# Two transformer blocks with a product-key expert layer: 32 instead of 16 of 128 first keys computed densely

## The reference, cut to what matters

```
q = (t @ wq).reshape(T, 8, 2, 128)          # 256 tokens, 8 heads, two halves
s1, s2 = q[:, :, 0] . k1, q[:, :, 1] . k2   # scores of 128 first and 128 second keys
v1, i1 = top_k(s1, 16); v2, i2 = top_k(s2, 16)
sc, pos = top_k(v1[..., :, None] + v2[..., None, :], 16)
idx = i1 * 128 + i2 at pos                  # expert number, of 16384
g = softmax(sc)
act = gelu(einsum('thkd,td->thk', u[idx], t))
out = einsum('thk,thkd->td', g * act, v[idx])
```

## Time and profile before

| | |
|---|---|
| three runs | 2838.87 us median (2834.85, 2838.87, 2839.47) |
| the profiled execution's own time | 2835.17 us |
| its span in the profile | 2833.4 us |
| busy share of the span | PE 85%, DVE 61%, ACT 50%, POOL 33% |
| granted TensorE clock, mean | 0.941 |
| HBM read | 809.09 MB |
| indirect gathers (queue q0) | 475.38 MB |

### The profile page before, as it was taken

One profiled execution on the slowest core, in us unless ns is written; L12 is line 12 of the kernel. 1 busy time (PEld: TensorE's weight loads), 2 busy tenths in 40 slices (PEclk: granted clock), 3 DMA queues, 4 the chain that ended last, 5 costly groups with the idle time before them and its releaser, 6 DMA issues.

```text
span 2833.4 us, 37176 instructions
## 1 busy us (share of the span) xinstructions
PE 2406.3 (85%) x14973; PEld 2079.6 (73%) x14973; DVE 1716.1 (61%) x2428; ACT 1421.4 (50%) x1692; POOL 926.2 (33%) x731
## 2 busy tenths in 40 slices
PE   8999999999999999999999677777766767777756
PEld 7887898888888788778888566666666666565654
DVE  4767564555456555577556877666647874444455
ACT  5567555544776444455554455444444444333443
POOL 6013150000000000432002646465446766344454
PEclk9999999999999999999999889898987778999977
DMA  7544404555445546334446999999999999999988
GB/s 229 190 142 153 137 16 146 165 195 193 150 133 185 183 129 223 119 119 161 156 162 227 380 374 403 410 400 413 406 409 381 402 385 413 415 398 412 416 347 337
DMA packets 209660, 751.84 MB, mean 265 GB/s; under 512 B 25133, under 2 KB 29449, under 8 KB 150857
## 3 DMA queue, kind: packets, MB, share of 16 engines
q0 software_dynamic: 74400, 475.38, 41.7%
q1 hardware_dynamic: 135088, 274.09, 28.2%
HBM read 809.09 MB, written 2.10 MB: 286 GB/s over the span
## 4 chain that ended last, share of the span: by engine, by line
DMA 28%; PE 21%; DVE 9%; issue 4%; POOL 4%; ACT 2%; POOLq 0%; DVEq 0%; ACTq 0%
DMA UROW<-in_peer_u_dram,WORK 20%; PE bank L2243 19%; DMA VROW<-in_peer_v_dram,WORK 7%; DVE BIG L2181 5%; POOL VROW L679 2%; POOL UROW L671 2%; PE bank L2898 1%; ACT VROW L1332 1%; DVE BIG L1741 0%; DVE WL L1441 0%; DMA UROW<-in_peer_v_dram,WORK 0%; DVE UROW L2181 0%; PE bank L2379 0%; ACT WH L799 0%; DVE WORK L1764 0%
## 5 line engine op out<-in xcount | busy, mean ns | idle before, releaser
L2898 PE MATMUL bank<-ID,VROW 128*128 128x128 f32 x3904 | 578.6, 312 | 373.6 <-ACT VROW L1332 373.4
L2181 DVE CUSTOM_DVE_ANT_0 BIG<-UROW,BIG 128x2048 f32<-128x2048 f32 x252 | 578.1, 2294 | 429.8 <-DMA UROW<-in_peer_u_dram,WORK 413.4
L2898 PEld LDWEIGHTS bank<-ID,VROW 128*128 128x128 f32 x3904 | 516.7, 161 | 429.1 <-ACT VROW L1332 421.9
L1332 ACT ACTIVATE VROW<-VROW,WORK 128x2048 f32<-128x2048 f32 x244 | 487.9, 2001 | 630.3 <-DMA VROW<-in_peer_v_dram,WORK 630.3
L2243 PE MATMUL bank<-HX,WH 128*128 128x512 f32 (+1 forms) x2784 | 759.5, 345 | 12.0 <-issue 4.8
L2243 PE MATMUL bank<-HX,WL 128*128 128x256 f32 x2128 | 595.5, 280 | 0.0
L671 POOL DMA_INDIRECT UROW<-in_peer_u_dram,WORK x256 | 340.2, 1329 | 631.3 <-DVE WORK L2181 408.3
L2243 PEld LDWEIGHTS bank<-HX,WH 128*128 128x128 f32 x2784 | 479.9, 189 | 84.1 <-issue 16.7
L1447 DVE TENSOR_TENSOR WL<-RAW,WH 128x1024 fp32r<-128x1024 f32 (+2 forms) x261 | 305.2, 1180 | 298.3 <-ACT WH L799 297.3
L2243 PE MATMUL bank<-WH,HX 128*128 128x512 f32 (+1 forms) x1472 | 453.1, 390 | 3.4 <-ACT BIG L742 2.5
L2243 PEld LDWEIGHTS bank<-HX,WL 128*128 128x128 f32 x2128 | 402.1, 189 | 0.1
(11 more groups left out here) (394 smaller groups left out, 2345.0 us busy)
## 6 DMA issues: line engine op xcount, KB each, us to landing
RAW<-in_w_in_odd_dram SPq DMA_DIRECT2D x64, 1024.0 KB, 5.3
RAW<-in_w_in_even_dram SPq DMA_DIRECT2D x48, 1024.0 KB, 5.3
RAW<-in_w_in_dram SPq DMA_DIRECT2D x44, 1024.0 KB, 5.0
RAW<-in_w_out_even_dram SPq DMA_DIRECT2D x16, 1024.0 KB, 5.1
RAW<-in_w_out_odd_dram SPq DMA_DIRECT2D x16, 1024.0 KB, 5.1
RAW<-in_w_out_dram SPq DMA_DIRECT2D x16, 1024.0 KB, 5.1
RAW<-in_peer_wq_dram SPq DMA_DIRECT2D x16, 1024.0 KB, 5.0
DROW<-in_peer_u_dram SPq DMA_DIRECT2D x32, 512.0 KB, 8.0
```

The lines of the kernel that those rows point to most:

```text
L1332: act.activation(v_buffer(n), v_buffer(n), ACT.Copy, scale=COEF[:, n:n + 1])\
L2181: dve.tensor_tensor_reduce(out=product, in0=UROW[:, b, :], in1=TT[m], op0=ALU.mult, op1=ALU.add, scale=1.0, scalar=0.0, accum_out=DOT[:, n ...
L2898: ins = pe.matmul(bank[c // 4][:, c % 4 * P:(c % 4 + 1) * P], v_buffer(n)[:, c * P:(c + 1) * P], ID[:, :], start=pick == 0 and c % 4 == 0, ...
```

## The change

`DENSE` becomes 32, so that experts with a first key of 96 or more (not 112) are computed densely and their rows aren't gathered. U_STEPS and V_STEPS become 128 each. The first dense steps lie on picks 2 to 115 (before: 2 to 108), the gate groups on 119 to 151 (112 to 155), the second dense steps on 155 to 233 (161 to 224). The search of block 1 takes 32 steps over picks 37 to 83, two in three picks, instead of one every second pick up to 99. ACTED has four parts instead of two, and takes BIG 4 to 12: the buffer JUNK is gone (the dot product now writes its product over the row), and the one-hots move from BIG into HT, whose first writing waits for the last dense dot. ACT waits for the searches ahead of the 17th and the 25th key, not the 9th. mix works in four parts instead of two. ADD_DENSE_AT, SUM_AT and SCALE_AT move from 108, 113 and 121 to 115, 119 and 124 picks into block 1 (236, 241, 249 to 243, 247, 252).

```diff
--- before.py
+++ after.py
@@ -44,7 +44,7 @@
 PICKS = PE_HEADS * PE_TOP
 ROWS_EACH, SECOND_ROWS = 4, 5
 V_LAG = 8
-DENSE = 16
+DENSE = 32
 KEPT = PE_KEYS - DENSE
 U_STEPS, V_STEPS = 4 * DENSE, 4 * DENSE
 GROUPS, IN_GROUP = 16, 16
@@ -52,7 +52,7 @@
 BATCH = 4
 N_PICKS = MT * PICKS
 ADD_AT = PICKS + 11
-ADD_DENSE_AT, SUM_AT, SCALE_AT = PICKS + 108, PICKS + 113, PICKS + 121
+ADD_DENSE_AT, SUM_AT, SCALE_AT = PICKS + 115, PICKS + 119, PICKS + 124
 ON_DVE = (N_PICKS - 7, N_PICKS - 5, N_PICKS - 4, N_PICKS - 2)
 TURNED = N_PICKS - 12
 BACK_AT = tuple(PICKS + 2 * g for g in range(4))
@@ -63,7 +63,6 @@
 TOP_STEPS = 8
 TOP_PLACES = (0, 1, 3, 4, 6, 8, 10, 12)
 TOP_LATER = (10, 20, 28)
-TOP_AT, TOP_EVERY = 37, 2
 TOP_INSIDE = TOP_STEPS
 GATES_AT = 116
 
@@ -73,10 +72,11 @@
     return {i: first + i * (last - first) // steps for i in range(steps)}
 
 
-U_AT = spread(U_STEPS + 1, 2, 109)
-G_TURN_AT = 110
-G_AT = spread(GROUPS, 112, 158)
-V_AT = spread(V_STEPS, 161, 226)
+TOP_BLOCK_1 = spread(4 * TOP_STEPS, 37, 85)
+U_AT = spread(U_STEPS + 1, 2, 116)
+G_TURN_AT = 117
+G_AT = spread(GROUPS, 119, 154)
+V_AT = spread(V_STEPS, 155, 234)
 G_PARTS_AT = G_TURN_AT + V_LAG + 1
 OH_AT = {g: v + V_LAG - 1 for g, v in G_AT.items()}
 MIX_AT = {g: v + V_LAG + 2 for g, v in G_AT.items()}
@@ -389,14 +389,14 @@
         GATE = WORK[:, 1024:1280]
 
         TT = [BIG[:, 2 * m:2 * m + 2, :].rearrange("p a b -> p (a b)") for m in range(MT)]
-        JUNK = BIG[:, 6:8, :].rearrange("p a b -> p (a b)")
         LNF = BIG[:, 0:2, :].rearrange("p a b -> p (a b)")
         UT = BIG[:, 15, :].rearrange("p (b n) -> p b n", b=2)
 
-        ACTED = [BIG[:, 4:6, :].rearrange("p a (j t) -> p (a j) t", t=T), BIG[:, 8:10, :].rearrange("p a (j t) -> p (a j) t", t=T)]
-        OH2 = BIG[:, 10:12, :].rearrange("p a b -> p (a b)").bitcast(BF16).rearrange("p (b t n) -> p b t n", b=2, n=P)
+        ACTED = [BIG[:, 4 + 2 * i:6 + 2 * i, :].rearrange("p a (j t) -> p (a j) t", t=T) for i in range((DENSE + 7) // 8)]
+        one_hot = HT[:, :, :].rearrange("p a b -> p (a b)").bitcast(BF16)
+        OH2 = one_hot[:, 0:4096].rearrange("p (b t n) -> p b t n", b=2, n=P)
         g_bf = BIG[:, 12:14, :].rearrange("p a b -> p (a b)").bitcast(BF16)
-        OH1 = g_bf[:, 0:2048].rearrange("p (b k t n) -> p b k t n", b=2, k=4, n=DENSE)
+        OH1 = one_hot[:, 4096:4096 + 8 * IN_GROUP * DENSE].rearrange("p (b k t n) -> p b k t n", b=2, k=4, n=DENSE)
         GATE_PARTS = g_bf[:, 2048:2816].rearrange("p (k t) -> p k t", k=3)
         I1T, I2T, IOTA_B = g_bf[:, 2816:3072], g_bf[:, 3072:3328], g_bf[:, 3328:3456]
         G_REST = BIG[:, 13, 768:1024]
@@ -1289,8 +1289,8 @@
             def dense_gelu(j):
 
                 act.wait_ge(s["d_m"], 4 * (j + 1))
-                if j == 8:
-                    act.wait_ge(s["tk_idx"], 4)
+                if j in (16, 24):
+                    act.wait_ge(s["tk_idx"], 4 if j == 16 else 8)
                 act.activation(ACTED[j // 8][:, j % 8, :], bank[6 + j % 2][:, 0:T], ACT.Gelu)\
                     .then_inc(s["d_act"], 1)
 
@@ -2124,6 +2124,9 @@
             def one_hots(g):
 
                 b, ts = g % 2, slice(IN_GROUP * g, IN_GROUP * (g + 1))
+                if g == 0:
+
+                    dve.wait_ge(s["d_m"], U_STEPS)
                 if g >= 2:
                     dve.wait_ge(s["g_g"], g)
 
@@ -2144,9 +2147,9 @@
                 dve.wait_ge(s["g_g"], g + 2)
                 dve.wait_ge(s["d_act"], DENSE)
                 gates_of = bank[6 + g % 2][:, 0:IN_GROUP * DENSE].rearrange("p (t a) -> p a t", a=DENSE)
-                for half in range(2):
-                    x = ACTED[half][:, :, IN_GROUP * g:IN_GROUP * (g + 1)]
-                    ins = dve.tensor_tensor(x, x, gates_of[:, 8 * half:8 * half + 8, :], ALU.mult)
+                for part in range(len(ACTED)):
+                    x = ACTED[part][:, :, IN_GROUP * g:IN_GROUP * (g + 1)]
+                    ins = dve.tensor_tensor(x, x, gates_of[:, 8 * part:8 * part + 8, :], ALU.mult)
                 ins.then_inc(s["g_mix"], 1)
 
             def root(m):
@@ -2177,8 +2180,7 @@
                 dve.wait_ge(s[f"u_row{b}"], 16 * (n // ROWS_EACH + 1))
                 if n >= 1:
                     dve.wait_ge(s["u_dot"], n)
-                product = UROW[:, b, :] if n < ROWS_EACH else JUNK
-                dve.tensor_tensor_reduce(out=product, in0=UROW[:, b, :], in1=TT[m], op0=ALU.mult, op1=ALU.add, scale=1.0,
+                dve.tensor_tensor_reduce(out=UROW[:, b, :], in0=UROW[:, b, :], in1=TT[m], op0=ALU.mult, op1=ALU.add, scale=1.0,
                                          scalar=0.0, accum_out=DOT[:, n:n + 1]).then_inc(s["u_dot"], 1)
                 for i, at in enumerate(TOP_LATER):
                     step = step_at(n, at, 1, TOP_STEPS)
@@ -2189,8 +2191,7 @@
                 i = step_at(n, 22, 8, 3)
                 if i is not None:
                     gates(0, 1 + i, 1)
-                step = step_at(n, TOP_AT, TOP_EVERY, 4 * TOP_STEPS)
-                if step is not None:
+                for step in steps_at(TOP_BLOCK_1, n):
                     top_part(1, step // TOP_STEPS, step % TOP_STEPS)
                 if n == GATES_AT:
                     gates(1, 0, 4)
```

## The result

The changed kernel takes 2847.9 us in the median of 13 runs, the kernel before 2837.9 in as many: a ratio of 1.0029 (95% interval 1.0018 to 1.0039). By the medians it is 10 us slower, by the ratio 8 (5 to 11), where 29.5 us less were forecast. One of the changed kernel's runs took 5884.0 us in a slow state and does not count in the ratio; the other twelve lie between 2837.2 and 2853.6 us, wider apart than those of the kernel before (2834.9 to 2840.9). The profiled execution took 2850.33 us with a span of 2848.3, against 2835.17 and 2833.4: 15.2 us more. All that follows by stretches is against these two.

What follows compares the result with a forecast made beforehand. DMA transfers were taken to bound the expert stage. -78.5 (bytes) + 6 (first dense part) + 36 (gate part) + 12 (second dense part) - 5 (end) = -29.5 us, forecast 2808 us; range 2772 to 2848, the forecast's own 2788 to 2828.

Steps and rivals of the forecast that it cites:

- What the change takes away and adds on the DMA: Expert stage: dropped rows -166.7 us, added dense loads +85.2, tiny packets +3; sum -78.5 us if the DMA stays full.
- First dense part: Picks 10 to 124: DMA sets 4.65 us a pick, PE and DVE mostly covered; +6 us (0 to 28).
- Gate part: Picks 126 to 161: DVE becomes the bound at 5.0 us a pick, where the DMA asks 3.90; +36 us.
- rival 3: Gate part: GpSimd's issues bind it, +50 to +97 us instead of +36, total about 2838; chance 0.17.
- Second dense part: Picks 155 to 233: PE waits for late loads into two half-row buffers, 5.20 us a pick; +12 us.
- the other bound: Second dense part by DMA alone: 3.90 us for a pick's gathers plus 1.08 for dense steps, 4.98 a pick.
- 5.14: Second dense part: least pace in us a pick that the two half-row buffers allow.
- Rival 2: Second dense part: half-row loop decides, kernel slower if landings average over 9.0 us; at 9.5, 2856 us; chance 0.15.
- The end: Around the sum of squares: DVE's 13.76 us stall shrinks to some 5, add_dense just isn't late; -5 us (-9 to +4).
- Rival 1: Whole expert stage: DMA stays the bound everywhere, -62 us, about 2776; chance 0.16.

Runs made afterwards that it cites:

- 24 keys: Changed kernel with DENSE = 24: 2833.6 us; with six halves, the gate part spread as in the kernel before and the changed kernel's end: 2831.4 us.
- the even drop: Changed kernel with every fourth token's row dropped in each gather, the fourth moving on with the picks, instead of rows by key: 2789.2 us, ratio 0.9836.
- the uneven drop: Changed kernel with 25% of the rows dropped, all from 32 tokens within partitions 64 to 127, instead of rows by key: 2992.3 us, ratio 1.0545.
- the spread part: Changed kernel with six halves and the gate part over picks 107 to 150 instead of 119 to 151: 2826.0 us; with the even drop too, 2761.2 us.
- six halves: Changed kernel with six half-row buffers for dense v rows instead of two, four of them in HT: 2827.9 us; with the even drop too, 2757.6 us.
- the search run: Changed kernel with the second block's search at every second pick again (to pick 99): 2845.4 us, ratio 1.0028.
- the first experiment: Kernel before, with rows of first keys 96 and up dropped from the gathers, its dense part unchanged: 2742.9 us, ratio 0.966.
- the second: Changed kernel, still gathering the rows of first keys 96 to 111 with zero coefficient: 2924.4 us, ratio 1.0308.

## Why the prediction was wrong

**The bytes** (step "What the change takes away and adds on the DMA"). Counts were right to 0.3 MB. The price of the dropped ones was not: 2.45 us per MB, taken from the traffic as a whole, against 1.71 measured for the very rows that were dropped. Over the 116 picks of the first dense part that is 30.8 MB x 0.74 = 23 us, and 22 are missing there. This is the step that failed. What the runs showed in its place: the worth of a dropped byte depends on where the dropped rows lie, 1.71 us per MB as the keys fall and 2.34 where every engine loses alike; that a buffer waits for the fullest engine is the reading of it, argued above. By the 1.71 the first part at 24 keys comes to 4.97 - 0.21 + 0.16 = 4.92 us a pick, which is what it took. The dense loads' price was right (0.33 a pick against 0.35).

**First dense part, the engines.** Right that neither PE (its clock rose to 0.99 as the gaps closed), nor DVE, nor the search, nor ACT's waits set the pace: the even drop leaves all their work as it is and takes 4.46 a pick, below the 4.65 of the forecast.

**Gate part.** Right: DVE is the bound, 4.94 against 5.0, and it stays there whatever the gathers do (4.95 with 68 MB more, 4.96 with the even and 4.99 with the uneven drop). The 3.90 that the forecast takes for the DMA alone no run reaches: with the rows dropped and the old dense part it is 4.37, and 4.32 with every fourth dropped evenly. One group of the changed kernel in DVE's order of time, as the earlier trace rows:

```profile
2231.37 2.29 DVE L2139 TENSOR_TENSOR HT<-BIG 128x2048 bf16<-128x2048 bf16 x1
2233.57 0.68 DVE L2140 TENSOR_TENSOR HT<-BIG 128x512 bf16<-128x512 bf16 x1
2234.29 1.90 DVE L2142 TENSOR_TENSOR HT<-HT,BIG 128x512 bf16<-128x512 bf16 x3
2236.10 0.15 DVE L2090 TENSOR_TENSOR WORK<-WORK,AMB 128x4 f32<-128x4 f32 x1
2236.17 2.30 DVE L2183 CUSTOM_DVE_ANT_0 UROW<-UROW,BIG 128x2048 f32<-128x2048 f32 x1
2238.40 0.08 DVE L2183 DVE_READ_ACCUMULATOR2_ANT WORK<- 128x1 f32 x1
2238.40 0.87 DVE L2152 TENSOR_TENSOR BIG<-BIG,bank 128x128 f32<-128x128 f32 x4
2239.20 2.28 DVE L2183 CUSTOM_DVE_ANT_0 UROW<-UROW,BIG 128x2048 f32<-128x2048 f32 x1
```

OH2 2.20, then 0.72 for the first and 1.81 for the other three OH1 operations, mix 0.80: 5.53 us, which is the sum made. That GpSimd comes close behind (rival 3) was right too, and is what kept the spread part from paying. Whether the part's excess over the DMA's need can be won at all stays open; no run kept both DVE and GpSimd off it.

**Second dense part.** The mechanism was right, the size too small. PE waits for a half row that lands, and GpSimd for PE (totals, times and longest in 2403 to 2700 us):

```profile
POOL VROW L679 <- PE bank L2899: 84.7, 36, 6.1
...
PE bank L2244 <- DMA DROW<-in_peer_v_dram: 29.8, 24, 3.5
```

PE in order of time around one such wait:

```profile
2509.72 1.02 PE L2244 MATMUL bank<-DROW,BIG 128*128 128x512 f32 x2
2510.58 1.05 PE L2244 MATMUL bank<-BIG,DROW 128*128 128x128 f32 x8
2513.70 1.12 PE L2244 MATMUL bank<-DROW,BIG 128*128 128x512 f32 x2 [2.07 <-DMA DROW<-in_peer_v_dram]
2514.66 1.05 PE L2244 MATMUL bank<-BIG,DROW 128*128 128x128 f32 x8
```

The dense loads of that stretch, from issue to landing:

```profile
DMA to landing us min/median/max: 4.1/7.8/9.9
```

After the second step of a half at 2511.6 us PE stands 2.07 us for the next half row. The landing was near the 7.9 us assumed, but the pace came to 5.36, not 5.20. The sum took for the other bound the DMA's 4.98 by the wrong price; with six halves, where the loop is gone, the part still takes 5.12. That 5.14 and 5.12 close together give more than either is argued, not shown, and the size isn't firm: the quick execution of the search run had 5.22. Rival 2 (the loop decides, slower) named the mechanism that tipped the balance, but with a landing over 9.0 us as its condition, which did not come.

**The end.** The stall at the sum was to shrink to 5 us for -5; alone it does so for -9, 138.6 us from pick 232 on instead of 147.1. In the changed kernel it didn't pay at all: 147.5. DVE waits for PE at add_dense (ten picks of distance were not "just not late") and then for the squares:

```profile
2767.05 2.48 DVE L2104 TENSOR_TENSOR XR<-XR,bank 128x512 f32<-128x512 f32 x4 [3.98 <-PE bank L2244]
...
2782.77 0.16 DVE L2158 TENSOR_REDUCE SM<-SM 128x1 f32<-128x4 f32 x1 [3.62 <-ACT BIG L1264]
```

Those are 3.98 + 3.62 us. With the six halves the end comes back, to 133.9. So the half-row loop had 20 us in it, not the 12 of the sum.

Together: 22 us in the first part by the price of a dropped byte, some 8 in the second part and 16 in the last row by the half-row loop and the same price, whose shares weren't taken apart there: 46 us less 2 us in the gate part, and 44.4 were missed between the profiled executions. Rival 1 (all DMA) was worth little for the same reason. The chance of 0.16 for slower was too low: every stretch was priced with one number, and no case was given to its being wrong.

## What to carry to other kernels

As far as this kernel shows, a price per byte read from a saturated queue is the price of bytes that leave all DMA engines alike; for rows that drop out at random, count what the fullest engine keeps, not the mean. When a change relieves the engine that bounds a kernel by a few per cent, list which loops had slack only because of it: here a two-buffer load loop, and a read at the end that it made late, took back 20 us, and four more half-row buffers in memory that was free turned a loss of 10 us into a gain of 10. A part spread out to free one engine can find the next one full: look at the sum of issue time and fixed gaps before moving it.

## What the runs showed of the hardware

- The DMA share hides part of the unevenness. It read 1.02 at 415 GB/s (the even drop), 0.98 at 383 (the changed kernel) and 0.88 at 331 (the uneven drop) for packets of the same sizes; the GB/s by slice told the first two apart.
- A dropped row still leaves one small packet: those under 512 B went from 25133 to 34462, 9329 more. Of these 8,306 are the dropped rows (the first experiment alone has 33439) and 1,023 come with the 64 further loads (the second has 26156). Before, as on the page:

```profile
DMA packets 209660, 751.84 MB, mean 265 GB/s; under 512 B 25133, under 2 KB 29449, under 8 KB 150857
```

- The HBM counter counts dropped rows as read. It rose by 33.55 MB, all of it the dense loads, though 68 MB of rows were no longer moved; and the kernel before with 68 MB fewer rows (the first experiment) read the same 809.09 MB as without:

```profile
HBM read 809.09 MB, written 2.10 MB: 296 GB/s over the span
```
